# Plain transposes of x between GEMMs, with the norm's root applied to the next GEMM's result

## The reference

```python
def rms_norm(x, g):
    y = x * lax.rsqrt(jnp.mean(x * x, axis=-1, keepdims=True) + EPS)
    return y * g
# block 1
proj = rms_norm(x, pre_mix_norm) @ w_in
mix = ...                                    # differential attention and NSA attention
x = x + rms_norm(mix @ w_out, post_mix_norm)
u = causal_dwconv(rms_norm(x, pre_ffn_norm) @ w_up, conv_w, conv_b)     # 3 taps along the tokens
gate, up = jnp.split(u, 2, axis=-1)
x = x + rms_norm((gelu(gate) * up) @ w_down, post_ffn_norm)
# block 2
proj = rmsnorm(x, mix_pre_gain) @ w_in_2
mixed = ... @ w_out_2                        # sliding window attention and a gated recurrence
x = x + rmsnorm(mixed, mix_post_gain)
u = relu(rmsnorm(x, mlp_pre_gain) @ w_up_2)
x = x + rmsnorm((u * u) @ w_down_2, mlp_post_gain)
```

## Time and profile before

| | us |
|---|---|
| median of 3 runs | 2612.89 |
| lowest and highest | 2609.93, 2614.18 |
| span of the profiled execution | 2603.2 |
| busy: TensorE matmuls, weight loads | 2440.9, 2054.4 |
| busy: VectorE, ScalarE, GpSimd | 1418.9, 1154.4, 81.2 |
| up1a, 12 blocks | 576.4 to 847.9 |
| out1 to up1a: no TensorE work, then the turn | 555.6 to 567.4, 567.4 to 576.4 |
| bytes read from HBM over the span | 415.52 MB, 160 GB/s |

### The profile page before, as it was taken

The page is one execution under the profiler, slowest core; times in us unless marked ns, Lnnn a source line. Parts: engine busy times, 40 slices in busy tenths (PEclk is TensorE's granted clock), DMA queues, the critical chain, the costliest instruction groups (busy, mean ns, idle before and its releaser), DMA issues.

```text
span 2603.2 us, 34397 instructions
## 1 busy us (share of the span) xinstructions
PE 2440.9 (94%) x12224; PEld 2054.4 (79%) x12224; DVE 1418.9 (55%) x1718; ACT 1154.4 (44%) x1620; POOL 81.2 (3%) x77
## 2 busy tenths in 40 slices
PE   6999987889999999999979996869899999999997
PEld 5887886768888788888868885658788888888886
DVE  4444336556666545666554445885555544455544
ACT  4444224445555444554444444334444444444432
POOL 1000100000000000000000001320000000000000
PEclk9999758989999999999989998889899999999999
DMA  7665330545555565665656652004466566665663
GB/s 228 193 191 163 98 129 5 166 130 186 186 185 175 190 192 171 193 193 193 191 159 189 193 161 65 1 25 153 128 186 185 186 192 190 190 185 182 208 193 105
DMA packets 298549, 418.71 MB, mean 161 GB/s; under 512 B 15263, under 2 KB 181465, under 8 KB 297701
## 3 DMA queue, kind: packets, MB, share of 16 engines
q1 hardware_dynamic: 295744, 407.09, 50.5%
q0 software_dynamic: 2144, 8.40, 1.0%
q10 hardware_dynamic: 580, 2.20, 0.2%
HBM read 415.52 MB, written 2.12 MB: 160 GB/s over the span
## 4 chain that ended last, share of the span: by engine, by line
PE 84%; issue 8%; DVE 5%; ACT 2%; POOL 1%; DMA 0%; ACTq 0%; DVEq 0%; POOLq 0%
PE PS L1289 22%; PE PS L1257 14%; PE PS L1256 14%; PE PS L1255 14%; PE PS L1290 11%; PE PS L1367 2%; PE PS L1302 1%; PE PS L1528 1%; DVE x L930 1%; DVE attT L1195 1%; DVE proj L1188 0%; PE PS L1304 0%; DVE proj L1192 0%; PE PS L1407 0%; PE PS L1344 0%
## 5 line engine op out<-in xcount | busy, mean ns | idle before, releaser
L806 DVE TENSOR_TENSOR wlo<-stage,whi 128x1024 fp32r<-128x1024 f32 (+2 forms) x452 | 540.3, 1199 | 625.1 <-ACT whi L529 625.0
L1289 PE MATMUL PS<-actT,whi 128*128 128x512 f32 x2432 | 859.7, 397 | 0.0
L529 ACT ACTIVATE whi<-stage 128x1024 fp32r<-128x1024 f32 (+2 forms) x452 | 467.2, 1037 | 679.6 <-PE PS L1257 656.4
L1290 PE MATMUL PS<-actT,wlo 128*128 128x256 f32 x2432 | 683.4, 281 | 0.0
L1289 PEld LDWEIGHTS PS<-actT,whi 128*128 128x128 f32 x2432 | 457.2, 188 | 112.9
L835 DVE TENSOR_TENSOR wlo<-stage,whi 128x1024 fp32r<-128x1024 f32 x298 | 358.5, 1223 | 232.5 <-ACT whi L580 230.3
L1290 PEld LDWEIGHTS PS<-actT,wlo 128*128 128x128 f32 x2432 | 456.5, 188 | 0.1
L580 ACT ACTIVATE whi<-stage 128x1024 fp32r<-128x1024 f32 x298 | 309.0, 1055 | 271.1 <-PE PS L1290 256.7
L1257 PE MATMUL PS<-whi,actT 128*128 128x512 f32 (+2 forms) x992 | 384.5, 388 | 0.0
L1255 PE MATMUL PS<-whi,actT 128*128 128x512 f32 (+2 forms) x992 | 383.8, 387 | 0.0
L1256 PE MATMUL PS<-wlo,actT 128*128 128x512 f32 (+2 forms) x992 | 381.7, 385 | 0.0
(11 more groups left out here) (249 smaller groups left out, 1605.3 us busy)
## 6 DMA issues: line engine op xcount, KB each, us to landing
stage<-in_w_up SPq DMA_DIRECT2D x304, 512.0 KB, 4.3
stage<-in_w_down SPq DMA_DIRECT2D x216, 512.0 KB, 4.7
stage<-in_w_in SPq DMA_DIRECT2D x168, 512.0 KB, 3.5
stage<-in_w_out SPq DMA_DIRECT2D x64, 512.0 KB, 4.8
stage<-in_cmp_k_w SPq DMA_DIRECT2D x8, 512.0 KB, 4.1
stage<-in_cmp_v_w SPq DMA_DIRECT2D x8, 512.0 KB, 5.1
x<-in_x ACTq DMA_DIRECT2D x2, 1024.0 KB, 6.9
grow<-bias_by_distance POOLq DMA_DIRECT2D x2, 1024.0 KB, 7.7
```

Source lines behind the costliest of these rows:

```text
L529: nc.scalar.activation(whi[:, s % SPLITS, 0:wd], stage[:, s % STAGES, 0:wd], ACT.Copy)\
L806: nc.vector.tensor_tensor(wlo[:, s % SPLITS, 0:wd], stage[:, s % STAGES, 0:wd], whi[:, s % SPLITS, 0:wd].bitcast(F32), ALU.subtract).then_ ...
L1289: nc.tensor.matmul(o, whi[:, j % SPLITS, at], actT[:, k, :], start=k == 0, stop=False)
L1290: last = nc.tensor.matmul(o[:, S:2 * S], wlo[:, j % SPLITS, at], actT[:, k, 0:S], start=False, stop=k == KC - 1)
```

## The change

Three of the four turns, n2, n3 and n4, become plain transposes of x with the identity, and no longer wait for the root. They wait for `resid`: the first 16 for the two pieces of the left half (of both token tiles), the other 16 for the right half; the order of the pieces is changed for it (`PIECES`). The squares and the variance stay, but stand behind `split_turned` on ScalarE and VectorE, and ScalarE's squares write to `yacc` instead of PSUM. The root is applied later: in in2 as the scale of ScalarE's copy out of PSUM (it waits for `rstd`), in up1 and up2 by a GpSimd multiply of 128x1024 on the joined sums of each block. There the tokens lie along the row, so GpSimd first writes the roots to DRAM and reads them back as a row on all partitions (`root_rows`). The readers of the joined sums wait for the new semaphore `pre_scaled`: `first_tap` on ScalarE in up1, `product` on VectorE in up2.

```diff
+            def root_rows(n, k):
+                pool.wait_ge(ev("rstd"), n)
+                for t in range(TT):
+                    pool.dma_start(roots[t].rearrange("(p o) -> p o", o=1), small[:, 4 + t:5 + t]).then_inc(ev("roots_out"), 16)
+                pool.wait_ge(ev("roots_out"), 16 * TT * k)
+                if k > 1:
+                    pool.wait_ge(ev("pre_scaled"), G["up2a"].acc)
+                row = roots.rearrange("t p -> (t p)").rearrange("(o s) -> o s", o=1)
+                pool.dma_start(root_row[:, :], row.broadcast_to((P, S))).then_inc(ev("row_in"), 16)
+
+            def scale_rows(name, conv):
+                g = G[name]
+                to = pre[:, :, 2:2 + S] if conv else lowsum
+                pool.wait_ge(ev("row_in"), 16 if conv else 32)
+                row = root_row[:, :].rearrange("p (o s) -> p o s", o=1).broadcast_to((P, 4, S))
+                with pool.Fori(0, g.blocks) as i:
+                    pool.wait_ge(ev("pre_done"), i + (g.acc + 3))
+                    pool.tensor_tensor(to, to, row, ALU.mult).then_inc(ev("pre_scaled"), 1)
...
             inv_sqrt(4, small[:, 4:6], small[:, 2:4], 2)
+            root_rows(4, 1)
+            scale_rows("up1a", True)
+            scale_rows("up1b", True)
...
             inv_sqrt(10, small[:, 4:6], small[:, 2:4], 2)
+            root_rows(10, 2)
+            scale_rows("up2a", False)
+            scale_rows("up2b", False)
...
# ScalarE, the copy of in2's result out of PSUM
-                        last = nc.scalar.activation(dst[:, t, span(col, wd)], PS[:, 4 * g.turned + 2 * bank + t, 0:wd], ACT.Copy)
+                        rs = small[:, 4 + t:5 + t] if name == "in2" else 1.0
+                        last = nc.scalar.activation(dst[:, t, span(col, wd)], PS[:, 4 * g.turned + 2 * bank + t, 0:wd], ACT.Copy, scale=rs)
...
# ScalarE, first_tap in up1
-                    act.wait_ge(ev("pre_done"), i + (g.acc + 3))
+                    act.wait_ge(ev("pre_scaled"), i + (g.acc + 1))
...
# ScalarE (n2 shown; n3 and n4 alike)
             tok("out1", "squares", then_first="up1a")
+            split_turned("n2")
             squares_of_x(1)
-            split_turned("n2")
...
# VectorE, product in up2
-                        dve.wait_ge(ev("pre_done"), i + (g.acc + 3))
+                        dve.wait_ge(ev("pre_scaled"), i + (g.acc + 1))
...
# VectorE, root_of_x: no diagonal matrices for n2, n3, n4
+                if k > 1:
+                    return
                 dve.wait_ge(ev("rstd"), n)
...
# TensorE
-                pe.wait_ge(ev(ready), n)
+                if ready != "resid":
+                    pe.wait_ge(ev(ready), n)
                 for c in range(KC):
+                    if ready == "resid" and c % 8 == 0:
+                        pe.wait_ge(ev("resid"), n + (c // 8 + 1) * TT)
...
-            turn("n2", "diag", 4)
+            turn("n2", "resid", 0)
```

## The result

The changed kernel takes 2627.51 us, median of five runs (2622.97 to 2631.39), against 2612.89 of the kernel before beside it: a ratio of 1.0061, with a 95% interval from 1.0043 to 1.0080. It is slower by 14.6 us. The forecast was +36.5 us. The direction came out as forecast, and the time lies in the range, but the size is that of rival (1), 2632, which was given 23%.

A forecast was written before the change was run, and what follows sets the result against it. TensorE was taken to bound the long stretches, the serial chain the three short turns. Turns -26.5, chain +41, tails +5 and clock +17 gave +36.5 on the median 2612.9: 2649 us, range 2624 to 2674.

The forecast's parts named there:

- rival (1): Up1 stalls: all as forecast, but gaps of 2 us are too short to lower the clock; +19.5, 2632 us; 23%.
- The turns, -26.5: Before up1a, in2 and up2a: transposes wait only for the residual, gaining 8.2, 9.4 and 8.9 us.
- The chain in up1, +41: Up1 block ends: multiply between join and first tap delays tile 4's wlo, 20 stalls of 2.05 us.
- The tails, +5: First blocks of down1a and down1b: TensorE already waits there, so the whole delay counts, 2 x 2.48 us.
- The clock, +17: Behind the up1 stalls: half of the 20 bring a fall to half clock, 1.7 us each; ends 0 and 34.
- up2 hidden: In up2 the multiply lies beside wlo of tiles 4 and 5, ahead of the product; cost 0.
- The root row hidden: Root row's two DMA trips by DRAM end just before up1a's first tap; late by 3 us once at worst.
- (2): Rival: the multiply is hidden and the gain at the turns stays; 2586 us; 4%.
- (3): Rival: contention with VectorE makes GpSimd's multiply take 3.6 us; +80, 2693 us; 8% together with (4).
- (4): Rival: late tile 3 and late root row eat the turns' whole 26.5 us; 2676 us; 8% together with (3).

The follow-up runs named there:

- the turns alone: The changed kernel without GpSimd's multiply by the root in the four up-projections, so that part of the computation is missing; 2582.27 us, 0.9890 of before.
- the series: The changed kernel with extra GpSimd work ahead of each up1 multiply: 16 columns, 128, or 128 twice; 2640.02, 2649.49 and 2658.81 us.
- the second experiment: The kernel before, old turns kept, plus a GpSimd multiply by a row of ones between join and first tap in up1; 2659.33 us, 1.0187 of before.

## Why the prediction was right or wrong, point by point

**The turns, -26.5: right in size, in part by luck.** Measured -27.6 by stage (-8.0, -9.9, -9.7). What sets the start was another thing than the one named. Weight tile 3 was to decide the start at 8.8 us. It did not: ScalarE's four squares follow each other every 1.04 us, the accumulator's read beside the next square, and took 4.16 us where 4.8 were reckoned, and whi of tile 3 was done 15.5 us after the residual's start, forecast 15.9, and wlo at 16.8, while TensorE wanted the tile at 17.5. What set the start was the 32 transposes at half clock. The two bounds happened to lie at 8.8 and 9.0. With the turns alone, where up1a starts at 7.5, tile 3 does come late, by 0.3 us.

ScalarE's timeline in the kernel after: the third and the fourth square, and tile 3's split (the first of three merged):

```profile
579.17 1.07 ACT L593 ACTIVATE yacc<-x 128x1024 f32<-128x1024 f32 x1
...
580.21 1.06 ACT L593 ACTIVATE yacc<-x 128x1024 f32<-128x1024 f32 x1
...
581.25 2.96 ACT L611 ACTIVATE whi<-stage 128x1024 fp32r<-128x1024 f32 x3
```

**The chain in up1, +41: right in mechanism and place, a little large.** Measured +38.1, 1.91 us a block instead of 2.05. The multiply was reckoned at 2.38 us by size from the 128x896 row, and measured 2.20 in up1; the handoffs came to 0.38 in all, 0.14 more than the single one of before, forecast 0.1. Together, 0.18 less and 0.04 more, that is the 0.14 by which 1.91 is under 2.05. The groups of instructions give both kinds of multiply (busy, mean ns):

```profile
L458 POOL TENSOR_TENSOR pre<-pre,root_row 128x1024 f32<-128x1024 f32 x22 | 48.4, 2198 | 616.5 <-DVE pre L872 616.5
L458 POOL TENSOR_TENSOR grow<-grow,root_row 128x1024 f32<-128x1024 f32 x16 | 38.4, 2398 | 487.7 <-DVE grow L872 487.7
```

**The tails, +5: right, a little small.** The waits doubled from 2.40 to 4.68 us, and the half clock behind them from 3.4 to 6.8 us in each, so +6.4 in all. The wait in the timeline of the kernel after:

```profile
884.03 0.80 PE L1288 MATMUL PS<-whi,gT 128*128 128x512 f32 x1 [4.68 <-DVE wlo L837]
```

Busy by stretch around it:

```profile
882.00:889.00 7.00, 4.97 (x12) 3.92 (x13) 5.13 (x5) 3.56 (x4) 0.00 (x0) 0.55 0.46 149
```

**The clock, +17: this is the step that failed.** It said "I take half of the 20, 10 x 1.7 = 17 us"; it measured 0, and this term alone makes 17 of the 22 us by which the forecast was too high. The chain adds 3 and the turns 1, the tails take back 1.4, and some 2 us are the difference between the stages (+17.2) and the medians (+14.6). Each fall does cost about what was said (1.5 us, forecast 1.7), and at the gap that the prediction reckoned with its count was near too: 8 of 20 at 2.04 us, forecast 10. But the gap came out at 1.84 instead of 2.05, mostly because the multiply took 2.20 us and not 2.38, and there the count was 0 of 20. The step put a price of 17 us on a quantity that goes from nothing to ten falls between 1.84 and 2.2 us, while the gap was known to no better than 0.2 us. The two rows (1.95 us of work in 3.5, no fall; 1.23, fall) left both cases open, and half of the falls was a middle between them. Rival (1) came about, though not for its reason that gaps of 2 us are too short: at 2.04 they are not.

By the page "TensorE: Matmul & The Clock Gate" of the Trainium skill, section "HAM oscillation — how this bites in real kernels", no gap of this length lowers the clock. The kernel after agrees (0 of 20), the series does not (8, 10 and 13 of 20 at 2.04, 2.22 and 2.57 us), and nor do two gaps of 1.95 us in the second experiment. The measurement decides, and it was right not to build on the rule, if not to take half.

**up2 hidden: right.** The stages are the same to 0.02 us. GpSimd and VectorE do lie side by side there, and it is VectorE that is stretched, two wlo in 4.22 us instead of 2.35, with the product behind them in time, as the timeline of the kernel after shows:

```profile
1969.39 2.40 POOL L458 TENSOR_TENSOR grow<-grow,root_row 128x1024 f32<-128x1024 f32 x1 [20.22 <-DVE grow L872]
1969.78 4.22 DVE L866 TENSOR_TENSOR wlo<-stage,whi 128x1024 fp32r<-128x1024 f32 x2 [0.47 <-ACT whi L611]
1973.93 1.22 DVE L896 SCALAR_TENSOR_TENSOR grow<-grow 128x1024 f32<-128x1024 f32 x1
```

**The root row hidden: right.** GpSimd's wait for the DRAM trip was 7.43 us (forecast 7.3), the row's load was issued at 591.41, and the first multiply, at 602.23, waited for the join and not for the row:

```profile
591.41 0.55 POOL L448 DMA_DIRECT2D root_row<-root_rows  x1 [7.43 <-DMA root_rows<-small]
...
602.23 2.20 POOL L458 TENSOR_TENSOR pre<-pre,root_row 128x1024 f32<-128x1024 f32 x1 [10.27 <-DVE pre L872]
```

**The rivals.** (2), the multiply hidden and 2586 us, needed a delay under 1.6 us; it was 2.33. With the tile moved ahead the multiply is hidden, at 2572 us, as the waits in down1a and down1b go too. (3), contention in the chain, did not come, as VectorE has nothing to do there. (4) did not come, all of the gain at the turns was kept.

## What to carry to other kernels

An operation put between two engines' steps delays every operation that stands behind the waiting instruction in a queue by its whole length, handoffs included, and the bound engine pays that less the room it had (here 2.33 less 0.43 us). What to ask first is which of those operations the bound engine waits for: here the 38 us lost in up1 came back by moving tile 4 ahead of the wait, 1.2 us of VectorE's time in each block, and none of it by making anything faster. Where a queue is idle ahead of a wait and late behind it, the order is wrong. A forecast that depends on a threshold should give the quantity and its error first; if the error spans the threshold, the two sides are two cases and no half of each.

## What the runs showed of the hardware

- Half clock behind a short gap of TensorE in a dense stream: none of the 20 gaps in the kernel after (17 of them 1.83 to 1.89 us, one 1.99), none of 18 at 0.82 or 0.83 with VectorE's multiply, two of three at 1.95 but not one of 2.25 in the same kernel, 8 of 20 at 2.04, 10 at 2.22, 13 at 2.57. In the series each costs 1.5 us, and equal gaps differ in whether one follows. The same wait of 2.4 us in down1a is followed by half clock in the kernel before and not in the one with the turns alone.
- The same 32 transposes behind the same idle time of 6.4 us took 6.63 us in the kernel after and 5.13 in the one with the turns alone, at granted clocks of 0.53 and 0.65.
- On GpSimd the fp32 multiply of two operands of 128x1024 takes 2.20 us in up1 (on `pre`) and 2.40 in up2 (on `lowsum`). A neighbour on VectorE is not the reason: with tile 4 first, up1's has wlo beside it and still takes 2.20. Where GpSimd starts first, VectorE's operation is the one stretched, from 1.22 to 2.89 us. Why up2's takes 0.2 us more stays open. A GpSimd operation of 128x16 took 0.215 us and one of 128x128 0.399.
- VectorE does the same multiply in 1.22 us.
- Stages that no edit touched, the two mixers, vary by 7.5 and 6.5 us over the ten profiled executions, one of each kernel, more than several of the differences looked for; the table by stage tells them apart, the total can't.
